# Two fused transformer-like blocks on one core: scan parameters fetched on ScalarE's queue, norms and mixers put ahead of weight halves

## The reference, cut to what matters

```
hn   = rmsnorm(h, norm1_g);  u, q, k, v, g_ssm, g_att = split(hn @ w_in)
y    = s5_mixer(u)                       # complex diagonal scan over tokens
o    = diff_attention(rmsnorm(q), rmsnorm(k), v)
h    = h + (sigmoid(g_ssm) * (y @ w_ssm_out) + sigmoid(g_att) * (rmsnorm(o) @ w_att_out)) @ w_o
h    = h + conv_glu_ffn(rmsnorm(h, norm2_g))
```

```
dt = exp(log_dt);  mag = exp(a_re * dt)
lb = mag * (cos(a_im * dt), sin(a_im * dt))
f  = (lb - 1) / a        # complex;  bb = f * b;  powers of lb follow
```

## Time and profile before

| | |
|---|---|
| median of 3 runs | 788.51 us (784.54 to 788.64) |
| the profiled execution | 790.22 us, span of its instructions 788.5 us |
| mean granted TensorE clock | 0.97 of full |
| busy, share of the span | PE 94%, PEld 87%, DVE 68%, ACT 48%, POOL 4% |
| chain that ended last | PE 74%, DVE 15%, ACT 5%, issue 3%, SP's queue 3%, DMA 1% |
| weight high half, mean | 1.91 us (106 times) |
| weight low half, mean | 2.29 us (106 times) |
| a weight unit, issue to landing, median | 5.0 to 5.6 us |

### The profile page before, as it was taken

How to read it: one execution, slowest core, us unless ns; L and a number is a source line. 1 busy time by engine, 2 the same in 40 slices (tenths; PEclk the granted TensorE clock), 3 DMA queues, 4 the chain that set the end, 5 groups by cost and what they waited for, 6 DMA issues and landing times.

```text
span 788.5 us, 14718 instructions
## 1 busy us (share of the span) xinstructions
PE 740.3 (94%) x6198; PEld 689.6 (87%) x6198; DVE 532.7 (68%) x933; ACT 379.0 (48%) x565; POOL 30.2 (4%) x60
## 2 busy tenths in 40 slices
PE   4968899999999899999999989979999999999997
PEld 2968687999889899999999989878998899889985
DVE  4899945556477877767677688856568565565553
ACT  5754252764627443443443574358664443434341
POOL 6010000000000000000000140000000000000000
PEclk9999698999999999999999989989999999999999
DMA  8515221144334445644555435333335565556521
GB/s 242 170 59 161 86 76 56 55 153 146 131 106 161 161 161 200 225 164 162 200 174 182 159 113 196 107 107 108 108 107 184 167 211 166 195 174 213 165 104 54
DMA packets 94399, 115.69 MB, mean 147 GB/s; under 512 B 7923, under 2 KB 83884, under 8 KB 94332
## 3 DMA queue, kind: packets, MB, share of 16 engines
q1 hardware_dynamic: 94204, 114.61, 44.5%
q0 software_dynamic: 128, 0.13, 0.1%
HBM read 113.69 MB, written 1.05 MB: 146 GB/s over the span
## 4 chain that ended last, share of the span: by engine, by line
PE 74%; DVE 15%; ACT 5%; issue 3%; SPq 3%; DMA 1%; DVEq 0%; ACTq 0%
PE psum L1661 15%; PE psum L1662 15%; PE psum L1663 15%; PE psum L2189 4%; PE psum L2190 4%; PE psum L2191 4%; DVE w_lo L955 4%; PE psum L1942 3%; PE psum L1938 3%; PE psum L1940 3%; ACT w_hi L507 3%; SPq L343 2%; PE psum L1790 1%; DMA w_raw<-in_w_in_dram 1%; PE psum L1758 1%
## 5 line engine op out<-in xcount | busy, mean ns | idle before, releaser
L955 DVE TENSOR_TENSOR w_lo<-w_raw,w_hi 128x2048 fp32r<-128x2048 f32 x106 | 242.5, 2290 | 129.7 <-ACT w_hi L507 129.4
L507 ACT ACTIVATE w_hi<-w_raw 128x2048 fp32r<-128x2048 f32 x106 | 201.8, 1906 | 61.4 <-PE psum L2191 41.7
L1661 PE MATMUL psum<-x2n_hi,w_hi 128*128 128x256 f32 x400 | 117.1, 293 | 3.2 <-DVE x2n_lo L1381 3.2
L1662 PE MATMUL psum<-x2n_lo,w_hi 128*128 128x256 f32 x400 | 114.5, 286 | 0.0
L1663 PE MATMUL psum<-x2n_hi,w_lo 128*128 128x256 f32 x400 | 114.4, 286 | 0.0
L1661 PE MATMUL psum<-hs_hi,w_hi 128*128 128x256 f32 (+1 forms) x352 | 100.4, 285 | 2.9 <-DVE ff L968 2.9
L1663 PE MATMUL psum<-hs_hi,w_lo 128*128 128x256 f32 (+1 forms) x352 | 100.0, 284 | 0.0
L1662 PE MATMUL psum<-hs_lo,w_hi 128*128 128x256 f32 (+1 forms) x352 | 99.8, 284 | 0.0
L1661 PEld LDWEIGHTS psum<-x2n_hi,w_hi 128*128 128x128 f32 x400 | 78.0, 195 | 6.6 <-DVE x2n_lo L1381 4.2
L1662 PEld LDWEIGHTS psum<-x2n_lo,w_hi 128*128 128x128 f32 x400 | 78.2, 196 | 0.7
L1663 PEld LDWEIGHTS psum<-x2n_hi,w_lo 128*128 128x128 f32 x400 | 78.1, 195 | 0.0
(11 more groups left out here) (444 smaller groups left out, 1546.4 us busy)
## 6 DMA issues: line engine op xcount, KB each, us to landing
w_raw<-in_w_ff_dram SPq DMA_DIRECT2D x32, 1024.0 KB, 5.3
w_raw<-in_w_in_dram SPq DMA_DIRECT2D x28, 1024.0 KB, 5.3
w_raw<-in_w_up_dram SPq DMA_DIRECT2D x22, 1024.0 KB, 5.1
w_raw<-in_w_down_dram SPq DMA_DIRECT2D x11, 1024.0 KB, 5.0
w_raw<-in_w_o_dram SPq DMA_DIRECT2D x4, 1024.0 KB, 5.2
w_raw<-in_w_out_dram SPq DMA_DIRECT2D x4, 1024.0 KB, 5.1
w_raw<-in_w_ssm_out_dram SPq DMA_DIRECT2D x2, 1024.0 KB, 5.6
w_raw<-in_w_att_out_dram SPq DMA_DIRECT2D x2, 1024.0 KB, 5.1
```

The costliest lines, as they stand in the source:

```text
L507: A.activation(w_hi[:, u % NW, :], raw[:, u % NRAW, :], ACT.Copy).then_inc(sem("hi_ready"), 1)
L955: V.tensor_tensor(w_lo[:, u % NW, :], raw[:, u % NRAW, :], w_hi[:, u % NW, :].bitcast(F32), ALU.subtract).then_inc(sem("lo_ready"), 1)
L1661: T.matmul(out_, lh, rh, start=start, stop=False)
L1662: T.matmul(out_, lh, rl, start=False, stop=False)
```

## The change

Four parts.

1. *Start.* The four parameter loads go from SyncE, behind the first weight unit, to ScalarE as its first instructions; ScalarE waits for them before its exp. The meta tokens' square sum goes from ScalarE to VectorE. ScalarE's first Sqrt of a constant goes. TensorE turns the parameters before norm1_g. VectorE makes the angles ahead of the tokens' square sum, the scan's base `l1` ahead of the first low half, and the divisor and factors between the `xn_low` steps. The low half of unit 1 goes behind two of the four powers, that of unit 2 (k's first) behind `b_blk`.
2. *First norm of block 2.* The low half of hg_f goes ahead of the first residual pair; ScalarE's squares of tiles 4 to 7 go behind all x2n_hi; the sums go behind all x2n_lo; `x2_stat` goes from between the groups of hg_f to behind them.
3. *Mixers.* `m_norm` and `level` go ahead of low halves, on ScalarE the high half `two_after("ck", 1)` ahead of `m_exp(1)`; `m_norm(3)` ahead of the wait for a root.
4. *Output norms.* The sums of squares were kept by token in columns (8, 2 and 2 columns wide) and spread over partitions after the reciprocal (`hg_bc`, `row_bc`). Now matmuls with `ones` or `sel` give them already spread, 256 columns wide, on 128 partitions (hg: 4 partitions, spread by one matmul each). Roots and reciprocals are taken of 256 columns. `row_bc` goes. VectorE's `two_after("hg_g")`, the low half of the second w_out2 unit, goes from ahead of the products to their end.

```diff
                 if n == 0:
-                    par(sp, "ssm_in", log_dt[:, :], ins["ssm_log_dt"].to_broadcast([P, 32]))
-                    for name, key in (("a_re", "ssm_a_re"), ("a_im", "ssm_a_im"), ("ssm_d", "ssm_d")):
-                        par_rows(sp, "ssm_in", 1, PROWS[name] - PROWS["a_re"], key)
...
-            act.wait_ge(sem("constants"), CONSTANTS["small"])
-            A.activation(small[:, 1, 8:9], eps_col, ACT.Sqrt)
-            ss = small[:, 0, 0:3]
-            for t, rows, signal in ((0, META, "meta_in"), (1, P, "x_in0")):
-                act.wait_ge(sem(signal), 16)
-                A.activation(junk_x[0:rows, :], xtok[0:rows, t, :], ACT.Square,
-                             accum_out=small[0:rows, 0, t:t + 1]).then_inc(sem("x_sq"), 1)
-                act.wait_ge(sem("x_sq"), t + 1)
-            act.wait_ge(sem("x_sq2"), 1)
-            A.activation(small[:, 1, 0:3], ss, ACT.Sqrt, bias=eps_col, scale=1.0 / D).then_inc(sem("x_rms"), 1)
...
-            split_to(1)
...
+            par(act, "ssm_in", log_dt[:, :], ins["ssm_log_dt"].to_broadcast([P, 32]))
+            for name, key in (("a_re", "ssm_a_re"), ("a_im", "ssm_a_im"), ("ssm_d", "ssm_d")):
+                par_rows(act, "ssm_in", 1, PROWS[name] - PROWS["a_re"], key)
             act.wait_ge(sem("ssm_in"), 64)
...
+            act.wait_ge(sem("constants"), CONSTANTS["small"])
+            act.wait_ge(sem("x_in0"), 16)
+            A.activation(junk_x[:, :], xtok[:, 1, :], ACT.Square, accum_out=small[:, 0, 1:2]).then_inc(sem("x_sq"), 1)
+            act.wait_ge(sem("x_sq"), 1)
+            act.wait_ge(sem("x_sq2"), 2)
+            A.activation(small[:, 1, 0:3], small[:, 0, 0:3], ACT.Sqrt, bias=eps_col,
+                         scale=1.0 / D).then_inc(sem("x_rms"), 1)
             act.wait_ge(sem("s5p_v"), 2)
             A.activation(sm("sin"), sm("thr"), ACT.Sin).then_inc(sem("s5p_a"), 1)
             A.activation(sm("sinh_"), sm("thr"), ACT.Sin, scale=0.5).then_inc(sem("s5p_a"), 1)
...
+
+            def x2_square(m):
+                A.activation(sqs[:, m, :], x2[:, m, :], ACT.Square).then_inc(sem("x2_stat_sq"), 1)
+
             for m in range(8):
                 act.wait_ge(sem("x2_ready"), m + 1)
                 A.activation(x2n_hi[:, m, :], x2[:, m, :], ACT.Copy, scale=col("norm_mix", m)).then_inc(
                     sem("x2n_hi"), 1)
-                A.activation(sqs[:, m, :], x2[:, m, :], ACT.Square).then_inc(sem("x2_stat_sq"), 1)
+                if m % 2:
+                    x2_square(m // 2)
+            for m in range(4, 8):
+                x2_square(m)
             split_to(unit_at[("hg_q", 0)]["n"] + 1)
...
+            two_after("ck", 1)
             m_exp(1)
-            two_after("ck", 1)
...
+            act.wait_ge(sem("hg_stat"), 2)
+            A.activation(rsm2[:, :], banks[5][0:4, 0:256], ACT.Sqrt, bias=eps_col[0:4, :], scale=1.0 / 64).then_inc(
+                sem("hg_rms"), 1)
+            act.wait_ge(sem("yc_stat"), 4)
+            A.activation(rst3[:, :], banks[6][:, 0:256], ACT.Sqrt, bias=eps_col, scale=1.0 / 512).then_inc(
+                sem("yc_rms"), 1)
...
+            act.wait_ge(sem("ya_stat"), 2)
+            A.activation(rst2[:, :], banks[7][:, 0:256], ACT.Sqrt, bias=eps_col, scale=1.0 / 256).then_inc(
+                sem("ya_rms"), 1)
...
             dve.wait_ge(sem("constants"), CONSTANTS["small"])
-            dve.wait_ge(sem("x_in1"), 16)
-            V.tensor_tensor_reduce(xr[:, 2, :], xtok[:, 2, :], xtok[:, 2, :], 1.0, 0.0, ALU.mult, ALU.add,
-                                   small[:, 0, 2:3]).then_inc(sem("x_sq2"), 1)
+            x_squares(0, META, "meta_in")
+            param_cols(1)
+            s5_angles()
+            x_squares(2, P, "x_in1")
             dve.wait_ge(sem("x_rms"), 1)
...
+            s5_lambda()
+            split_to(1)
+            xn_low(0)
+            xn_low(1)
+            xn_low(2)
+            xn_low(3)
+            s5_denominator()
+            xn_low(4)
+            s5_factor(0)
+            xn_low(5)
+            s5_factor(1)
+            xn_low(6)
+            half_columns()
+            xn_low(7)
             power(parts(l_pow, 1), parts(l_pow, 0), parts(l_pow, 0), q1)
             power(parts(f_pow, 1), parts(f_pow, 0), parts(l_pow, 0), q1)
+            split_to(2)
             power(parts(l_pow, 2), parts(l_pow, 1), parts(l_pow, 0), q1)
             power([f_pow[:, i, 2:4, :] for i in range(2)], [f_pow[:, i, 0:2, :] for i in range(2)],
                   [l_pow[:, i, 1:2, :].to_broadcast([P, 2, NS]) for i in range(2)], [p_tmp[:, i] for i in range(4)])
-            split_to(3)
-
...
+            split_to(3)
...
+            lo_upto("hg_f")
             x2_pair(0)
-            lo_upto("hg_f")
             x2_pair(1)
             x2_low(0)
             x2_low(1)
             x2_pair(2)
             x2_low(2)
             x2_low(3)
-            x2_squares(2)
-            x2_low(4)
-            x2_low(5)
             x2_pair(3)
-            x2_low(6)
-            x2_squares(4)
-            x2_low(7)
-            x2_squares(6)
+            for m in range(4, 8):
+                x2_low(m)
+            for m in (2, 4, 6):
+                x2_squares(m)
             tt(rst3[:, :], sqs[:, 0, :], sqs[:, 1, :], ALU.add).then_inc(sem("x2_stat_sum"), 1)
...
+            m_norm(0)
+            scale("lru_x", 0, 1, lru_g[:, 1, :])
+            level(3)
             two_after("lru_x")
-            scale("lru_x", 0, 1, lru_g[:, 1, :])
-            m_norm(0)
-            level(3)
             lru_conv(1)
             scale("cq", 1, 0, cq[:, 2, :], 0.125)
-            two_after("cq", 1)
             level(4)
             scale("cq", 1, 1, cq[:, 3, :], 0.125)
             m_max(1)
+            two_after("cq", 1)
             scale("ck", 1, 0, ck[:, 2, :])
-            two_after("ck", 1)
             m_norm(1)
             level(5)
+            two_after("ck", 1)
             scale("ck", 1, 1, ck[:, 3, :])
             level(6)
...
+            m_norm(3)
             dve.wait_ge(sem("lru_s"), 2)
             seq(tt(lru_i[:, :, :], lru_i[:, :, :], lru_t[:, :, :], ALU.mult))
-            m_norm(3)
...
-            y_factor(1, sm("hg_rt", 8))
-            y_factor(2, sm("yc_rt", 2))
-            two_after("hg_g")
+            dve.wait_ge(sem("hg_rms"), 1)
+            V.reciprocal(rsm2[:, :], rsm2[:, :]).then_inc(sem("hg_r"), 1)
+            dve.wait_ge(sem("yc_rms"), 1)
+            seq(V.reciprocal(rst3[:, :], rst3[:, :]))
             scale("hg_g", 0, 0, hgg[:, 0, :])
...
             for p_ in range(4):
-                STT(out=mo[:, p_, :], in0=mo[:, p_, :], scalar=col("att_norm", p_), in1=banks[6][:, 0:256],
+                STT(out=mo[:, p_, :], in0=mo[:, p_, :], scalar=col("att_norm", p_), in1=rst3[:, :],
                     op0=ALU.mult, op1=ALU.mult).then_inc(sem("yc"), 1)
-                if p_ == 1:
-                    y_factor(3, sm("ya_rt", 2))
                 if p_:
                     y_low(p_ - 1, 3 + p_, mo[:, p_ - 1, :])
+            y_low(3, 7, mo[:, 3, :])
+            dve.wait_ge(sem("ya_rms"), 1)
+            seq(V.reciprocal(rst2[:, :], rst2[:, :]))
             for m in range(2):
+                STT(out=xc[:, m, :], in0=xc[:, m, :], scalar=col("lru_norm", m), in1=rst2[:, :],
+                    op0=ALU.mult, op1=ALU.mult).then_inc(sem("ya"), 1)
+            scale("hg_g", 0, 1, hgg[:, 1, :])
+            for m in range(2):
+                dve.wait_ge(sem("hg_bc"), m + 1)
...
+                y_low(4 + m, m, xc[:, m, :])
...
-                y_low(4 + m, m, xc[:, m, :])
             for m in range(2):
                 y_low(6 + m, 2 + m, hgo[:, m, :])
+            two_after("hg_g")
...
+            param_cols(1, "ssm_in", 4)
             param_cols(0, "par0_in", 1)
...
-            param_cols(1, "ssm_in", 4)
...
                 for m in range(2):
-                    for t in range(2):
-                        c = 4 * m + 2 * t
...
-                token_sums(banks[6], [(sq2, sq3)[p_ // 2][:, p_ % 2, :] for p_ in range(4)])
...
+                    pe.wait_ge(sem("hgo"), m + 2)
+                    T.matmul(banks[5][0:4, 0:256], sel[:, m, 0:4], hqf[:, m, :], start=(m == 0),
+                             stop=(m == 1)).then_inc(sem("hg_stat"), 1)
...
-            unit("hg_f", 0, x2n, 8, ready="x2n_lo", between=x2_stat)
...
+                    T.matmul(banks[7][:, 0:256], ones[:], hgk[:, m, :], start=(m == 0), stop=(m == 1)).then_inc(
+                        sem("ya_stat"), 1)
...
+                for p_ in range(4):
+                    pe.wait_ge(sem("yc_sq"), p_ + 1)
+                    T.matmul(banks[6][:, 0:256], ones[:], (sq2, sq3)[p_ // 2][:, p_ % 2, :], start=(p_ == 0),
+                             stop=(p_ == 3)).then_inc(sem("yc_stat"), 1)
...
+            unit("hg_f", 0, x2n, 8, ready="x2n_lo")
+            x2_stat()
...
-                row_bc(2, banks[6], sm("yc_rt", 2))
                 ya_stat()
...
```

(2 more changed lines are left out.)

198 lines of the change are left out of this document (81 added, 117 removed).

## The result

| | before | changed |
|---|---|---|
| median of the runs, us | 787.93 (784.54 to 788.64, 4 runs) | 770.91 (770.64 to 771.81, 4 runs) |
| ratio to before | 1 | 0.9777, 95% interval 0.9758 to 0.9797 |
| profiled execution: span, us | 788.5 | 768.9 |
| TensorE busy in it, us | 740.3 | 728.0 |

What follows compares the result with a forecast made beforehand. TensorE, busy 94% of the span, was taken as the bound, with time only in its waits and half clock. 6.5 + 4.0 + 7.3 + 1.1 + 0 = 18.9 us gave a forecast of 770, range 761 to 780.

Steps and rivals of the forecast that it cites:

- The start: Everything up to the scores in block 1: forecast to give 6.5 us, bounds 4.3 to 9.0.
- Sqrt after 11: Sign named in advance that the forecast is wrong: ScalarE's Sqrt after 11 us, pointing to the parameters.
- Parameters at 5.3, at most 6.7: Start: the four parameter loads on ScalarE's queue land between 4.7 and 6.7 us, taken as 5.3.
- parameters late: Rival, chance 0.15: parameters wait behind x and first weights, land as late as 9.9; 775 us, or 777.
- Sqrt at 9.0: Start, ScalarE: Sqrt comes at 9.0 us, against 8.11 in the kernel before.
- Second state-input step 5.5 us earlier: Start, TensorE: s5_in(1) starts 5.5 us earlier than its 81.25, as VectorE delivers sz at 75.7.
- Its half clock: Second state-input step, with no hole ahead, takes 4.22 us instead of 7.11: 2.9 us more gained.
- minus 2.5 for v's first unit: Start: half clock may move behind the sums of squares onto v's first unit; 2.5 us deducted, between 0 and 3.3.
- Opening norm: Norm that opens block 2: 4.0 us gained, half clock of 458 to 464 gone; bounds 2.0 to 4.6.
- Mixers: Block 2 mixers: 7.3 us from pairs 0 and 1, 1.1 us from pair 3; bounds together 5.5 to 9.5.
- Output norms: Block 2 output norms: 0 us, between -3.0 and +0.5; 4.7 us more reciprocals, about 2.4 us of broadcasts saved.
- slower: Rival, chance 0.03: low halves moved back become the bound, above all the second output unit's; 797 us.

Runs made afterwards that it cites:

- e7: Changed kernel with all four parameter loads moved from ScalarE's queue to SyncE's, behind the first weight unit; 773.52 us, ratio 0.9828.
- e12: Kernel before, with 34 unused matmuls put into TensorE's wait for sz ahead of the second state-input step; 785.92 us, ratio 0.9962.
- e1: Changed kernel with the start as in the kernel before, so only block 2 is changed; 776.09 us, ratio 0.9840.
- e2: Changed start only, block 2 as in the kernel before; 785.08 us, ratio 0.9960.
- e6: Changed kernel with the mixers' order of the kernel before; 782.41 us, ratio 0.9927.
- e8: On top of e4: ScalarE's eight copies of BT ahead of a weight half, exp of lambda moved earlier; 772.06 us, ratio 0.9790.
- e10: On top of e8: low half of k's first unit ahead of b_prod, v's low halves behind the state multiplies; 770.70 us, ratio 0.9763.
- e3: Changed kernel with the output norms of the kernel before; 771.03 us, ratio 0.9788.
- e4: Changed kernel with the norm of x ahead of the parameter work on ScalarE and VectorE; 770.12 us, ratio 0.9775.
- e5: Changed kernel with the norm that opens block 2 as in the kernel before; 776.42 us, ratio 0.9853.
- e9: Changed kernel with the low half of k's first unit back ahead of b_prod; 773.86 us, ratio 0.9803.

## Why the prediction was right in sum, and where it was wrong

**The start: 6.5 forecast, 5.0 found.** The sum is near by luck: its largest term failed nearly whole, and others, wrong the other way, hid it. One of the prediction's own signs of being wrong, Sqrt after 11, came true.
- *Parameters at 5.3, at most 6.7.* They landed at 7.87, later than both bounds, 5.7 us after the last one's issue began (2.20). The row that I went by, meta tokens 2.1 us after its issue, was first in its queue; the parameters were issued while x, a megabyte, was on its way. The rival "parameters late" had 9.9. e7 shows that on SyncE's queue it would have been 11.3. The rule of the Trainium skill ("DMA: Bandwidth & Descriptors", Issuing engines are not separate DMA queues), that only issue time is saved, is borne out but for 0.8 us: a queue of their own saved 3.4 us, and SyncE's later issue of the last one, done at 5.35 in e7 against 2.77, explains 2.6. That the queues share is seen at the meta tokens too, 3.3 us instead of 2.1. How much of the parameters' 5.7 us is due to x no run tells.
- *Sqrt at 9.0.* It came at 13.84. 2.6 us are the landing; 1.2 the angles, which took 2.7 us from 8.54 to 11.24; 1.3 the table load, which I had hidden behind the square sum. That load came only when ScalarE's wait for the square sum had ended (2.02 us idle, then the load at 12.55), while the load for Exp ran at 2.80, ahead of the wait for the parameters. Those three carry it to 14.1. The 1.5 us for the angles is what they take in the kernel before (23.41 to 24.92), dependences included; in the changed kernel single operations among them are longer:

```profile
9.18 1.08 POOL L434 TENSOR_SCALAR_AFFINE_SELECT selT<-selT 16x1024 f32<-16x1024 f32 x1
9.26 1.03 DVE L953 TENSOR_SCALAR small<-small 128x16 f32<-128x16 f32 x1
```

  The same operation took 0.17 us before (L972 at 23.70), where GpSimd was idle; here it ends with GpSimd's. The pair ahead of it took 0.68 us instead of 0.26, again up to the end of a GpSimd operation. In e7, where the angles run later, they took 1.9 us. No run moves GpSimd's work alone, so this cause is likely, not shown.
  By the Trainium skill ("ScalarE: Activation LUTs", What ACT_TABLE_LOAD costs) a drain of 1380 ns belongs to each switch; load at 12.55 and ACTIVATE at 13.84 show 1.29 in all, so the rows of before held.
- *Second state-input step 5.5 us earlier.* This is the step that failed: it is 0.5 earlier. TensorE was 4.1 us later than forecast at its first unit, 4.0 at k's, 5.2 at k's second, where the 2.6 us wait for BT is added, and 5.1 at this step (80.76 for 75.7); VectorE's `sz` came 4.2 later. The lateness of VectorE is that of its front: `b_prod` began at 30.88 where 27.0 was forecast. Both engines were late by about the same, so no hole opened: the wait of 4.7 us that is gone was paid by TensorE's working later, not won. The error of the front thus reached this term in full, 5.0 us of 5.5.
- *Its half clock.* 2.9 forecast, 2.9 found (7.11 to 4.2). The sums behind it gave 1.7, where I had put 0.6. And *minus 2.5 for v's first unit* did not come: 92 to 96 is at full clock.
So 0.5 + 2.9 + 1.7 = 5.1 stands in the place of 5.5 + 2.9 + 0.6 - 2.5: 5.0 too much, hidden by 1.1 and 2.5 too little. What the start gave is the clock, as e12 shows in the kernel before: with the step no earlier (0.9 later even) and the clock behind it kept up, 3.1 us of the time go.

**Block 1: 0 forecast, 1.7 found.** A half clock at 208 to 214 is missing in the changed kernel, after the same 1.1 us wait. e1, e2, e6, e8 and e10 to e12 have it (at 198 to 212), e3, e4, e5, e7 and e9 have not, and the code of that stretch is the same in all. "Elsewhere orders and durations are the same" was right for the orders alone. Kernels with the changed start show it both ways, so the 1.7 us can't be credited to the change.

**Opening norm: 4.0 forecast, 5.2 found.** In the times of the kernel before (6.7 us added, by which TensorE is ahead there), the last x2n_lo ended at 454.8 (455.2 forecast), hg_q started at 459.7 (460.0), cq's first unit at 466.1 (467.1). The half clock went. e5 shows it by the undoing.

**Mixers: 8.4 forecast with pair 3, 9.1 found.** m_norm(1) ran at 497.07, that is 509.0 in the times of before (11.9 added; 509.2 forecast); the scores behind hA kept 0.9 of a wait, 0.6 forecast. Both waits for `mp` went, the half clock behind the first too. e6 brings all of it back.

**Output norms: 0 forecast, 1.4 lost.** The saving of 2.4 us on TensorE was wrong. The statistics and broadcasts stand at three places in the kernel before, at two in the changed one:

```profile
557.67 0.95 PE L2020 MATMUL psum<-sel,hqf 128*128 128x2 f32 x8
...
564.80 1.09 PE L2045 MATMUL psum<-ident,small 128*64 128x128 f32 x16
...
570.13 0.60 PE L2053 MATMUL psum<-ident,small 128*128 128x128 f32 x4
```

```profile
536.77 1.03 PE L2040 MATMUL psum<-hqf,sel 128*4 128x256 f32 x4
537.73 1.99 PE L2101 MATMUL psum<-sq,ones 128*128 128x256 f32 x8
...
542.51 1.12 PE L2046 MATMUL psum<-rsm,selT 4*128 4x256 f32 x4
543.57 1.13 PE L2095 MATMUL psum<-hgk,ones 128*128 128x256 f32 x4
```

The next unit's matmuls start at 560.26, 567.19 and 570.49 before, at 539.37 and 544.35 now. So these steps took 5.3 us of TensorE's time and take 4.4: 0.9 saved. I had counted what is removed, not what is put in. The reciprocals (1.74, 1.68, 1.74 us) show as the 1.8 us wait for ycat_lo; that wait less the 0.9 saved makes 0.9 of the 1.4 lost, and the other 0.5 is not accounted for. The loss lies within the bounds given, -3.0 to 0.5. The moved low half cost nothing: no wait for it stands in the list, and "slower" had no hold.

So the gain of 19.6 us on the spans met the 18.9 forecast because the errors, -1.5, +1.7, +1.2, +0.7 and -1.4, nearly cancel; of these the first hides a term that was wrong by 5.0. The opening norm and the mixers were right in mechanism, and within 1.2 us in size; in the start only the step's own half clock was.

**What stays open.** The undone parts add up to more than the whole: e1, e5 and e6 cost 5.0 + 6.0 + 11.8 us, the change gave 17.6 (0.0223 of 788). Some of their stretches of half clock belong to no part. Why the clock falls in one trace and not in the other after the same wait stays open; so does the cause of the long operations among the angles.

## What to carry to other kernels

A wait of TensorE has two prices, its length and the half clock that may follow. The second can be the larger (in e10 3.4 us of half clock behind a wait of 2.5), so list the granted clock beside every wait before you cost it. Where the wait can't be removed, matmuls that nothing uses, put into a free bank, took the second price away: 18 of them gave 3.6 to 4.2 us. And when a chain is brought forward, follow each engine to the place where they meet: TensorE came to its second state-input step 4 us sooner in e10 than in e8 (73.6 for 77.6), yet the step began only 1.9 us sooner, as VectorE's `sz` was there at 76.0.

## What the runs showed of the hardware

The granted clock does not follow from the program alone. The kernel before ran at a mean clock of 0.979 in 785.33 us and at 0.972 in 788.4 on the same chip, e9 at 0.988 in 769.62 us and at 0.982 in 775.08. Stretches of half clock come and go, at 1.7 us each or twice that. The change, e2, e3, e5 and e6 are one program up to block 2, and their traces differ: the clock falls at 44 to 48 in the changed kernel (0.57), at 52 to 60 in e3, e5 and e6 (in e3 0.82 up to 56 and 0.75 from there on), and at both places in e2. The 2.6 us wait for BT, alike in the change and in e2, has full clock behind it in the one (1.00 at 56 to 60) and 0.58 in the other. With medians of five runs differences under some 2 us can't be told here, and a span of a single execution is no better.

Four small loads landed 3.4 us sooner from a second queue than from SyncE's behind the first weight unit (7.87 and 11.3, e7), of which 2.6 are the earlier issue. They still took 5.7 us from the last one's issue to its use, against 2.1 for the meta tokens of the earlier trace rows, and the loads issued beside them on the first queue came later: the meta tokens after 3.3 us instead of 2.1, and while the small loads were under way, at 2 to 4 us, the DMA engines moved 41 and 52 GB/s, where e7 has 111 and 303.

A small VectorE operation can take six times its usual time beside a GpSimd operation: 1.03 us for 0.17 in the changed kernel, 0.96 us for 0.26 (a pair) in e4. Each of these ended within 0.15 us of the end of a GpSimd operation on 16 partitions of 1024 elements.
